# Strassen's identity in nine of 22 tile pairs a block, neighbours two at a time, in place of five apart

## The reference

```
f = (silu(rms_norm(h) @ w_gate) * (rms_norm(h) @ w_up)) @ w_down     # 1024 -> 2816 -> 1024
h = h + 0.5 * rms_norm(f)
```

## Time and profile before

| | |
|---|---|
| median of 3 runs | 2000.92 us (2000.67 to 2001.42) |
| the profiled execution's own time | 2001.3 us |
| its span | 1999.5 us |
| granted TensorE clock | 0.999 |
| PE busy | 1986.0 us, 99% of the span, 15084 matmuls |
| DVE, ACT, POOL busy | 913.9, 824.6, 1029.3 us |

### The profile page before, as it was taken

One profiled execution on the slowest core, in us unless ns is written; L12 is line 12 of the kernel. 1 busy time (PEld: TensorE's weight loads), 2 busy tenths in 40 slices (PEclk: granted clock), 3 DMA queues, 4 the chain that ended last, 5 costly groups with the idle time before them and its releaser, 6 DMA issues.

```text
span 1999.5 us, 35699 instructions
## 1 busy us (share of the span) xinstructions
PE 1986.0 (99%) x15084; PEld 1909.5 (96%) x15084; DVE 913.9 (46%) x1433; ACT 824.6 (41%) x1318; POOL 1029.3 (51%) x1257
## 2 busy tenths in 40 slices
PE   9999999999999999999999999999999999999998
PEld 9999999999899999999999999999998998888887
DVE  6663310478546765210076542103785467642102
ACT  6433222465555533232264332224555465332321
POOL 3655554576315655454375554544763256564551
PEclk9999999999999999999999999999999999999999
DMA  4224332132201223332122333321322112333321
GB/s 167 86 94 125 103 102 86 67 96 80 64 33 43 85 85 127 100 117 88 57 75 85 96 117 111 102 84 62 101 82 65 33 54 74 109 124 107 116 73 43
DMA packets 48479, 175.76 MB, mean 88 GB/s; under 512 B 5184, under 2 KB 9408, under 8 KB 48320
## 3 DMA queue, kind: packets, MB, share of 16 engines
q1 hardware_dynamic: 48176, 173.40, 26.6%
q10 hardware_dynamic: 144, 0.10, 0.0%
HBM read 171.38 MB, written 2.10 MB: 87 GB/s over the span
## 4 chain that ended last, share of the span: by engine, by line
PE 98%; DVE 1%; ACT 1%; DMA 0%; issue 0%; SPq 0%; DVEq 0%
PE ps L1803 97%; PE ps L2184 1%; DMA h<-in_x 0%; DVE osb L1751 0%; ACT xh L829 0%; DVE xl L1761 0%; DVE tail_step L1295 0%; PE ps L2063 0%; DVE probT L1719 0%; ACT prob L1151 0%; DVE small L1728 0%; DVE h L1300 0%; ACT tmp L1187 0%; ACT xh L1202 0%; DVE wlo L1329 0%
## 5 line engine op out<-in xcount | busy, mean ns | idle before, releaser
L747 POOL TENSOR_TENSOR wlo<-raw,whi 128x256 fp32r<-128x256 f32 (+2 forms) x1148 | 944.0, 854 | 726.2 <-ACT whi L799 723.6
L1803 PE MATMUL ps<-xh,whi 128*128 128x264 f32 (+2 forms) x2680 | 645.3, 296 | 3.2 <-DVE xl L1334 1.5
L1803 PE MATMUL ps<-xl,whi 128*128 128x264 f32 (+2 forms) x2680 | 641.7, 295 | 0.0
L1803 PE MATMUL ps<-xh,wlo 128*128 128x264 f32 (+2 forms) x2680 | 640.8, 295 | 0.0
L1803 PEld LDWEIGHTS ps<-xh,whi 128*128 128x128 f32 x2680 | 445.0, 188 | 17.4 <-DVE wlo L1329 2.3
L799 ACT ACTIVATE whi<-raw 128x1024 fp32r<-128x1024 f32 (+3 forms) x329 | 356.0, 1083 | 255.7 <-PE ps L1803 221.6
L1803 PEld LDWEIGHTS ps<-xl,whi 128*128 128x128 f32 x2680 | 443.7, 188 | 11.4
L1803 PEld LDWEIGHTS ps<-xh,wlo 128*128 128x128 f32 x2680 | 443.6, 189 | 10.5
L1803 PE MATMUL ps<-hidh,whi 128*128 128x264 f32 (+2 forms) x1276 | 313.6, 296 | 0.0
L1803 PE MATMUL ps<-hidl,whi 128*128 128x264 f32 (+2 forms) x1276 | 312.5, 295 | 0.0
L1803 PE MATMUL ps<-hidh,wlo 128*128 128x264 f32 (+2 forms) x1276 | 312.4, 295 | 0.0
(11 more groups left out here) (218 smaller groups left out, 2332.8 us busy)
## 6 DMA issues: line engine op xcount, KB each, us to landing
raw<-in_ffn_up SPq DMA_DIRECT2D x88, 512.0 KB, 3.7
raw<-in_ffn_down SPq DMA_DIRECT2D x64, 704.0 KB, 4.0
raw<-in_ffn_gate SPq DMA_DIRECT2D x87, 512.0 KB, 3.6
raw<-in_w_in SPq DMA_DIRECT2D x28, 512.0 KB, 3.5
raw<-in_w_out SPq DMA_DIRECT2D x16, 512.0 KB, 3.6
raw<-in_w_q SPq DMA_DIRECT2D x8, 384.0 KB, 3.2
out_t<-h SPq DMA_DIRECT2D x16, 128.0 KB, 1.8
h<-in_x SPq DMA_DIRECT2D x2, 528.0 KB, 5.7
```

Source lines behind the costliest of these rows:

```text
L747: ins = nc.gpsimd.tensor_tensor(w_lo(n)[:, at], raw[:, r, at], w_hi(n)[:, at].bitcast(F32), ALU.subtract)
L1803: return nc.tensor.matmul(o, w, x, start=start, stop=stop)
```

## The change

STRASSEN becomes (4, 5, 7, 8, 10, 11, 13, 14, 16): nine pairs, of which eight stand side by side in twos, with a plain pair between the twos. When the next pair is a Strassen pair too, DVE makes the fourth weight sum, `sums(nxt[3])`, before `low(nxt[1])` and not after `up(m)`. As the first Strassen pair is now 4, the input sums are made one pair earlier: `sum_inputs(0)` stands before the loop over pairs, `t_sums(0)` stands in pair 0 (before: pair 1) and `t_sums(3)` in pair 2 (before: pair 3), and each `sum_hi` and `t_low` moves forward with them. The four `t_hi` and `t_lo` parts lie in unused columns of `whi`, `wlo` and `raw` and in chunks of the hidden tensor that are written later; all have the sizes as before.

```diff
--- before.py
+++ after.py
@@ -116,7 +116,7 @@
 DVE_TAIL = (0, 2, 4, 6, 7)
 
 
-STRASSEN = (5, 7, 9, 11, 13)
+STRASSEN = (4, 5, 7, 8, 10, 11, 13, 14, 16)
 KH = DC // 2
 T_SUMS = 4
 
@@ -129,7 +129,7 @@
     assert FC % 2 == 0 and FC >= 6
 
 
-    assert FC - DC > max(STRASSEN) and FC - DC - 4 > min(STRASSEN) > 4
+    assert FC - 5 > max(STRASSEN) and FC - 9 > min(STRASSEN) > 3 and FH >= DC + 3
 
 
     tiles = []
@@ -310,6 +310,7 @@
         xl = sb("xl", [P, DC, T], F32R)
         tail_step = sb_at("tail_step", xh_at, [P, DC, T], F32)
         f_ffn = sb_at("f_ffn", xl_at, [P, DC, T], F32)
+        raw_at = base[0]
         raw = sb("raw", [P, RING, MAXT * P], F32)
         whi = sb("whi", [P, RING, MAXT * P], F32R)
         wlo = sb("wlo", [P, RING, MAXT * P], F32R)
@@ -328,10 +329,36 @@
         hidh = sb_at("hidh", arena, [P, FC, T], F32R)
         hidl = sb_at("hidl", arena + FC * CH, [P, FC, T], F32R)
 
-        t_hi = sb_at("t_hi", arena + (FC - DC) * CH, [P, KH, T_SUMS, HALF], F32R)
-        t_lo = sb_at("t_lo", arena + (2 * FC - DC) * CH, [P, KH, T_SUMS, HALF], F32R)
-        t_in = sb_at("t_in", arena + (FC - DC - 4) * CH, [P, 2, T], F32)
-        t_sum = sb_at("t_sum", arena + (FC - DC - 2) * CH, [P, T_SUMS, HALF], F32)
+        hid_all = sb_at("hid_all", arena, [P, 2, FC, T], F32R)
+        raw_spare = sb_at("raw_spare", raw_at, [P, RING, MAXT * P], F32R)
+        spare = slice(DC * P, DC * P + HALF)
+
+        def four(first, which):
+            return hid_all[:, which, first:first + 2, :].rearrange("p a (i t) -> p (a i) t", i=2)
+
+        last = hid_all[:, :, FC - 1, :].rearrange("p a (i t) -> p a i t", i=2)
+        T_HI = [whi[:, :, spare], raw_spare[:, :, spare], four(FC - 5, 0), four(FC - 3, 0)]
+        T_LO = [wlo[:, :, spare], last, four(FC - 5, 1), four(FC - 3, 1)]
+
+        def t_half(part, k, nt):
+
+            at = part[k]
+            if at is last:
+                return at[:, :, :, 0:nt]
+            return at[:, :, 0:nt]
+
+        def t_one(part, k, i, nt):
+            at = part[k]
+            if at is last:
+                return at[:, i // 2, i % 2, 0:nt]
+            return at[:, i, 0:nt]
+
+        def t_whole(k, nt):
+            at = t_sum[:, :, 0:nt]
+            return at.rearrange("p (a i) t -> p a i t", i=2) if T_LO[k] is last else at
+
+        t_in = sb_at("t_in", arena + (FC - 9) * CH, [P, 2, T], F32)
+        t_sum = sb_at("t_sum", arena + (FC - 7) * CH, [P, T_SUMS, HALF], F32)
 
         off = [arena]
 
@@ -987,7 +1014,7 @@
                 def sum_hi(k):
                     act.wait_ge(t_sum_ready, KH * F + k + 1)
                     nt = span(trim, 0)[1]
-                    nc.scalar.activation(t_hi[:, k, :, 0:nt], t_sum[:, :, 0:nt], ACT.Copy).then_inc(t_hi_ready, 1)
+                    nc.scalar.activation(t_half(T_HI, k, nt), t_sum[:, :, 0:nt], ACT.Copy).then_inc(t_hi_ready, 1)
 
                 def part_copy(m):
 
@@ -998,6 +1025,7 @@
                     nc.scalar.activation(half(tmp[4], trim, 0), bank(FIRST_U[b, m], trim, 0), ACT.Copy)\
                         .then_inc(part_copied, 1)
 
+                sum_inputs(0)
                 for m in range(FC):
                     n = TILES_OF[b, m]
                     if m in STRASSEN:
@@ -1012,16 +1040,18 @@
                     if m:
                         hi(n[0] + RING)
                     if m == 1:
+                        sum_hi(1)
+                        sum_inputs(2)
+                    hid_hi(m)
+                    hi(n[1] + RING)
+                    if m == 0:
                         sum_hi(0)
                         sum_inputs(1)
-                    hid_hi(m)
-                    hi(n[1] + RING)
-                    if 0 < m < 4:
-                        sum_hi(m)
-                    if m < 3 and m != 1:
-                        sum_inputs(0 if m == 0 else 3)
                     elif m == 1:
-                        sum_inputs(2)
+                        sum_hi(2)
+                        sum_inputs(3)
+                    elif m == 2:
+                        sum_hi(3)
                 tables(LN_EXP_TABLES)
                 for m in range(DC - split[b]):
                     hi(out_slot(b, m) - 1 + RING)
@@ -1430,11 +1460,14 @@
                     chain.link(nc.vector.tensor_tensor(t2, b22, t1, ALU.subtract))
                     nc.vector.tensor_tensor(t4, b21, t2, ALU.subtract).then_inc(t_sum_ready, 1)
 
+                def t_high(k, nt):
+                    at = t_half(T_HI, k, nt).bitcast(F32)
+                    return at.rearrange("p (a i) t -> p a i t", i=2) if T_LO[k] is last else at
+
                 def t_low(k):
                     dve.wait_ge(t_hi_ready, KH * F + k + 1)
                     nt = span(trim, 0)[1]
-                    nc.vector.tensor_tensor(t_lo[:, k, :, 0:nt], t_sum[:, :, 0:nt],
-                                            t_hi[:, k, :, 0:nt].bitcast(F32), ALU.subtract).then_inc(t_lo_ready, 1)
+                    nc.vector.tensor_tensor(t_half(T_LO, k, nt), t_whole(k, nt), t_high(k, nt), ALU.subtract).then_inc(t_lo_ready, 1)
 
                 def sums(n):
 
@@ -1507,6 +1540,8 @@
                         sums(nxt[1])
                         low(nxt[0])
                         sums(nxt[2])
+                        if m + 1 in STRASSEN:
+                            sums(nxt[3])
                         low(nxt[1])
                         strassen_sums(m, 1)
                         strassen_sums(m, 2)
@@ -1514,26 +1549,31 @@
                         strassen_sums(m, 3)
                         gate(m)
                         up(m)
-                        sums(nxt[3])
+                        if m + 1 not in STRASSEN:
+                            sums(nxt[3])
                         hid(m)
                         low(nxt[3])
                         hid_lo(m)
                         continue
                     gate(m)
                     if m == 1:
-                        t_sums(0)
-                    elif 2 <= m <= 4:
-                        t_low(m - 1)
+                        t_low(0)
+                        t_sums(1)
+                    elif 2 <= m <= 3:
+                        t_low(m)
                     sums(nxt[1])
                     low(nxt[0])
                     up(m)
                     hid(m)
                     low(nxt[1])
                     hid_lo(m)
-                    if m == 1:
-                        t_low(0)
-                    if 1 <= m <= 3:
-                        t_sums(m)
+                    if m == 0:
+                        t_sums(0)
+                    elif m == 1:
+                        t_low(1)
+                        t_sums(2)
+                    elif m == 2:
+                        t_sums(3)
                     if b == 0 and m == FC - 4:
                         decay_rates()
                 output_sum(b)
@@ -1852,7 +1892,7 @@
                     return lambda k: (xh[:, k + upper * KH, at:at + nt], xl[:, k + upper * KH, at:at + nt])
 
                 def sums(i):
-                    return lambda k: (t_hi[:, k, i, 0:nt], t_lo[:, k, i, 0:nt])
+                    return lambda k: (t_one(T_HI, k, i, nt), t_one(T_LO, k, i, nt))
 
                 slot_in(n[0])
                 part(n[0], False, tokens(0, a0), bank(z, trim, 0), ug).then_inc(part_mm, 1)
```

## The result

The changed kernel takes 2030.33 us (2030.11 to 2030.55), the kernel before beside it 2000.83: a ratio of 1.0147, interval 1.0131 to 1.0163, so 1.5% slower. The profiled execution's span is 2028.6 us against 1999.5, 29.1 longer; +23 was forecast.

The account below looks back on a forecast made before the run. PE bounds the kernel, busy 1986.0 of 1999.5 us. Waits less gains give +4.45 us in each of blocks 0, 2, 3 and +9.7 in block 5, in all +23: 2024.0 us against 2000.92, range 2003 to 2038.

Parts of the forecast that it names:

- The gain: Four more Strassen pairs per block remove matmuls: 23.2 us gained if PE never waits, of which 5.0 in block 5.
- DVE and POOL taking turns: DVE operations with two SBUF inputs and POOL pieces exclude each other: a weight sum costs about 1.15 us, not 0.60.
- the walk: Dates of neighbouring Strassen pairs' steps followed through each engine's queue, compared with when PE wants each result, giving PE's waits.
- The couple: Two neighbouring Strassen pairs: PE waits 0.48 us for `gate` and 0.52 for the part copy; 1.0 together, 1.85 in block 5.
- The first couple: Pairs 4 and 5, where input sums run into the couple's work: PE waits 7.55 us a block, 9.2 in block 5.
- The six waits of the prediction: PE waits 1.04, 0.81 and 2.5 us in pair 4, then 1.8, 0.86 and 0.52 in pair 5.
- nothing else moves: Moved steps issue no DMA, SP's queue is late only as counted, mixers and output products stay: no further cost.
- The first couple loses little: Rival: later couples wait as forecast, but DVE gets through the input sums in time; -9 us, 1992; chance 0.1.
- Losses about equal the gain: Rival: the first couple costs half the forecast price, leaving the time within 0.2%; chance 0.06.
- DVE and POOL do not meet: Rival: without collisions only the first couple makes PE wait; 13.6 us gained, 1987, or 1978 without that wait; chance 0.07.
- More is lost: Rival: POOL is late with B's s2up low part, or slots drift; up to 3 us a couple, 2045; chance 0.12.

Follow-up runs that it names:

- the memset run: Changed kernel, but POOL fills the gate tile's low part in each couple's second pair by memsets of zeros, not subtractions reading SBUF: 2014.43 us.
- The cut input sums: Changed kernel with the input sums of feature groups 1 to 3 made for only 64 of 264 columns: 2023.6 us.
- two small moves: Changed kernel with seven pairs, and in each couple the second pair's s13 low part on POOL and its part copy before the first's silu: 1990.30 us.

## Why the prediction was right, and where its sizes were off

**The gain.** Forecast 23.2 us if PE never waits. It is not seen as a time by itself, but the rates hold to 0.13 us a couple: the 33.40 us from couple to couple less its two late starts and two restarts (0.59, 0.53, 0.20) are 32.08, and 32.21 were forecast. The delay against the kernel before, taken at the first matmul of each output phase (261.62 and 267.04 in block 0), grew by 5.42, 5.72, 6.52 and 11.49 us from block to block, 29.15 in all, as much as the span, so nothing moved outside the blocks. The waits are then 29.15 + 23.2 = 52.4 us net, where the prediction had 46.4.

**DVE and POOL taking turns.** Right, and shown by the memset run: with POOL's reads gone beside the sums `gate` is back at 10.98 us. The price in the walk was 1.15 us a sum beside POOL; the timeline has 1.22, 1.11 and 1.04, and 0.96 for the first. What the walk did not have is POOL's side of it: its four pieces took 4.17 us, not 2.82. It cost nothing here.

**The couple.** Forecast 1.0 us, measured 1.19 (33.40 against 32.21). PE's matmul behind the `gate` wait starts 0.59 after it was due, and 0.48 was forecast; the one behind the copy 0.53 against 0.52. On top come 0.10 us at each restart, for which the walk had no term. In block 5 the same distance, 1742.03 to 1775.23, is 33.20 against 11.13 + 2 x 9.88 = 30.89: 2.31, where 1.85 was forecast. The couples (7, 8) and (10, 11) have three waits there, not two: PE also waits 0.50 and 0.41 us for z (1742.03, 1775.23), for which the walk of a couple had no date.

**The first couple.** Forecast 7.55 us in block 0. Its gate and up phase grew from 234.34 to 240.12 us, by 5.78 (it began 0.36 us sooner, hence the 5.42 above). With the 6.1 gained it lost 11.9 in all and three couples 3.6 of it, so 8.3; by the run without pair 4 it is 7.9. The six waits of the prediction, 1.04, 0.81, 2.5, 1.8, 0.86 and 0.52, appear as 1.26, 0.65, 2.18, 1.74, 0.63 and 0.36 of idle time ahead of the rows; each matmul then starts 0.17 later than the idle time says, since that is counted from the end of the record ahead, 0.28 after its start, and the next was due 0.12 after it. So from due date to start they are 1.42, 0.82, 2.35, 1.89, 0.79 and 0.52. That is 7.8 in all; six restarts of 0.10 make it 8.4. Only the first wait is off by more than 0.15: the unit came free when the walk said (PE's next matmul at 61.32, 61.4 in the walk), but PE began pair 4 at 57.35 and not at 57.82. The cut input sums confirm what was said of its cause.

**Mis-sized term.** The waits came to 52.4 us in place of 46.4, so the time was 6 us above the forecast. Blocks 0, 2 and 3 lost 36.3 us where 31.65 were forecast, block 5 16.5 in place of 14.75; 0.36 came back at the start of block 0. The walks had no term for a restart: the fifty waits of the four rows, at 0.10 us each, are 5 us. The first wait of pair 4 was 0.4 us longer than forecast, and block 3's last couple has a wait of 0.48 for z that the walk did not have. In block 5 "nothing else moves" failed: a wait of 0.41 us for POOL's low part (1690.32) comes ahead of pair 4, like those of the run with the old five pairs. Somewhat shorter distances behind a wait give a part back, so these are no exact sum.

**The rivals.** "The first couple loses little" is out: it cost at least 7.2 us a block by the run without pair 4. "Losses about equal the gain" is out by the 1.5%. "DVE and POOL do not meet" is out by the timeline, and the memset run shows that the point from which it decides was rightly placed: with the meeting gone the couples of blocks 0 and 2 behind the first are free. "More is lost", up to 3 us a couple, is seen only in block 5, and there it is 2.3.

**What the prediction undersold.** The sooner fourth sum was told only as a place on DVE; the run with it late is 30 us slower, for the greater part through the SP queue. I had traced SP's queue for what the change delays, not for what the edit spares.

## What to carry to other kernels

An engine that is idle for half the span can still be the limit at the moment that counts: walk one round of the pattern through each queue, in order, with the durations that the operations have beside their neighbours, and compare the dates with those at which the bottleneck engine wants each result. Where two engines take turns at a port, spacing the work apart or moving one operation across may be worth more than the operation removed: here two small moves, with seven pairs in place of nine, made a loss of 1.5% into a gain of 0.5%. A buffer's last reader sets when its next load is issued, and with a queue in order it sets all those behind it too.

## What the runs showed of the hardware

**A restart costs 0.10 us.** In the PE rows above, the matmul behind a wait (111.21) is 0.39 us long in place of 0.28, and the next comes 0.23 us later in place of 0.12. It is so, to some hundredths, at every wait of the feed-forward blocks at the full clock (0.36 to 0.39 long, the next 0.19 to 0.23 later), however short: at 0.37 us of idle time (113.66) as at 2.18 (66.49).

**The clock fell in two of the four blocks, after the waits of pair 4.** The granted clock by stretches: us, PE busy (records), clock in parts of full speed, DMA share, GB/s.

```profile
66.00:69.00 3.00, 2.51 (x20) 1.00 0.54 172
690.00:693.00 3.00, 0.81 (x7) 1.00 0.58 175
694.00:697.00 3.00, 3.00 (x15) 0.50 0.32 124
1700.00:1704.00 4.00, 4.00 (x21) 0.50 0.40 131
```

At 0.50 TensorE runs at 1.2 GHz, otherwise at 2.4. In block 2 it had waited 1.41, 0.81 and 2.35 us between 685.8 and 692.4, and the clock was 1.00 at 690 to 693 and 0.50 at 694 to 697; matmuls are then 0.22 us apart and not 0.12. In block 0 the same three waits (61.32 to 66.49) were not followed by a fall. In block 5 it was down from 1697.2 to 1704.0. The two stretches at 0.50 are 10.2 us, so some 5 us of PE's time, but that is no part of the 29 in that size: DVE went on meanwhile, and the next wait was 0.29 us in block 2 in place of 1.89 in block 0. Over all runs, such stretches among or right behind pair 4's waits are found in every kernel that keeps the first couple, in one to four of its blocks, in block 0 too in four of the runs. The run with the fourth sum late has one more behind a later couple, where PE had just waited 3.0 us for z (1141.13). A kernel without the first couple, the one before included, has none but at the very end of the span. What decides in which blocks the clock falls is open.

**POOL gives and takes.** Beside the sums its pieces took 1.04 us each, beside nothing 0.70. The loss of one engine at the port is not the other's gain.
